# Loading the high parts of five weight chunks with a casting DMA from GpSimd instead of copying them on ScalarE

## What is computed

```python
kv = (rms_norm(h @ w_dkv)[..., :256] @ w_ukv).reshape(b, s, 16, 64 + 64)   # chunks ukv0, ukv1
k  = rope_tail(rms_norm(concat([k_nope, k_rope_of_all_heads]), k_gain), cos, sin)
q  = (rms_norm(h @ w_dq) @ w_uq).reshape(b, s, 16, 96)                     # chunks uq0 .. uq3
q  = rope_tail(rms_norm(q, q_gain), cos, sin)
logits = einsum('bqhd,bshd->bhqs', q, k) * 96 ** -0.5                      # 16 heads, masked by blocks of 64
out = einsum('bhqs,bshd->bqhd', softmax(logits), v)
h = h + out.reshape(b, s, 1024) @ w_o                                      # chunks bo0 .. bo3
h = h + square(relu(rms_norm(h) @ w_up)) @ w_down                          # chunks mlp1.u*, mlp1.d*
```

## Time and profile before

| | |
|---|---|
| time, median of 3 runs | 1129.64 us (1126.74 to 1129.78) |
| time of the profiled execution | 1127.46 us |
| its span, first to last instruction | 1125.7 us |
| TensorE's mean granted clock | 0.995 of full |
| TensorE busy | 1101.4 us, 98% |
| VectorE busy | 769.9 us, 68% |
| ScalarE busy | 601.3 us, 53% |
| GpSimd busy | 138.3 us, 12% |
| ScalarE's weight copies (line 1700) | 156 in one group, 290.1 us |

### The profile page before, as it was taken

One profiled execution on the slowest core, in us unless ns is written; L12 is line 12 of the kernel. 1 busy time (PEld: TensorE's weight loads), 2 busy tenths in 40 slices (PEclk: granted clock), 3 DMA queues, 4 the chain that ended last, 5 costly groups with the idle time before them and its releaser, 6 DMA issues.

```text
span 1125.7 us, 17842 instructions
## 1 busy us (share of the span) xinstructions
PE 1101.4 (98%) x7003; PEld 976.9 (87%) x7003; DVE 769.9 (68%) x1077; ACT 601.3 (53%) x778; POOL 138.3 (12%) x104
## 2 busy tenths in 40 slices
PE   8999999999999999999999999999999999999996
PEld 7868888888888888888889999898899989999995
DVE  6774665555668656565656878566688578988885
ACT  6574544444679555444455546455545357555552
POOL 3632100000275240000030000000000002000001
PEclk9999999999999999999999999999999999999998
DMA  9635565565342246656545654446643556654631
GB/s 344 237 115 114 177 200 194 183 201 187 107 146 96 76 130 224 198 188 193 187 151 185 202 169 127 145 150 215 216 155 127 165 209 225 218 174 170 223 131 38
DMA packets 138785, 194.00 MB, mean 172 GB/s; under 512 B 7147, under 2 KB 112840, under 8 KB 138716
## 3 DMA queue, kind: packets, MB, share of 16 engines
q1 hardware_dynamic: 126796, 181.92, 48.8%
q10 hardware_dynamic: 11312, 11.05, 3.5%
q0 software_dynamic: 608, 0.08, 0.0%
HBM read 191.90 MB, written 6.37 MB: 176 GB/s over the span
## 4 chain that ended last, share of the span: by engine, by line
PE 77%; DVE 7%; ACT 7%; DMA 4%; issue 3%; POOL 1%; SPq 0%; ACTq 0%; DVEq 0%; POOLq 0%
PE psum L616 19%; PE psum L617 19%; PE psum L618 19%; PE psum L825 9%; PE psum L826 5%; ACT arena L1686 4%; ACT whi L1700 2%; PE psum L704 2%; DMA skew_a<-tab_a 2%; DVE wlo L2314 2%; PE psum L1355 1%; PE psum L1382 1%; DMA raw<-in_a_w_in 1%; PE psum L734 1%; DVE arena L2840 1%
## 5 line engine op out<-in xcount | busy, mean ns | idle before, releaser
L2314 DVE TENSOR_TENSOR wlo<-raw,whi 128x2048 fp32r<-128x2048 f32 (+3 forms) x136 | 307.0, 2264 | 128.7 <-ACT whi L1700 127.7
L1700 ACT ACTIVATE whi<-raw 128x2048 fp32r<-128x2048 f32 (+3 forms) x156 | 290.1, 1868 | 187.1 <-PE psum L618 125.3
L616 PE MATMUL psum<-xA,whi 128*128 128x256 f32 x840 | 239.3, 285 | 0.1
L617 PE MATMUL psum<-xA,whi 128*128 128x256 f32 x840 | 237.6, 283 | 0.0
L618 PE MATMUL psum<-xA,wlo 128*128 128x256 f32 x840 | 237.6, 283 | 0.0
L1669 POOL TENSOR_TENSOR wlo<-raw,whi 128x288 fp32r<-128x288 f32 (+3 forms) x51 | 90.0, 1792 | 759.5 <-ACT whi L1700 759.4
L825 PE MATMUL psum<-xA,whi 128*128 128x512 f32 x512 | 181.9, 398 | 0.0
L616 PEld LDWEIGHTS psum<-xA,whi 128*128 128x128 f32 x840 | 160.3, 191 | 3.3 <-issue 1.2
L617 PEld LDWEIGHTS psum<-xA,whi 128*128 128x128 f32 x840 | 160.4, 191 | 1.1
L618 PEld LDWEIGHTS psum<-xA,wlo 128*128 128x128 f32 x840 | 160.3, 191 | 0.1
L826 PE MATMUL psum<-xA,wlo 128*128 128x256 f32 x512 | 143.7, 281 | 0.0
(11 more groups left out here) (302 smaller groups left out, 1673.5 us busy)
## 6 DMA issues: line engine op xcount, KB each, us to landing
raw<-in_w_in SPq DMA_DIRECT2D x42, 1024.0 KB, 4.9
raw<-in_mlp_w_up SPq DMA_DIRECT2D x32, 1024.0 KB, 5.2
raw<-in_mlp_w_down SPq DMA_DIRECT2D x32, 1024.0 KB, 4.8
raw<-in_w_gate SPq DMA_DIRECT2D x11, 1024.0 KB, 5.1
raw<-in_w_up SPq DMA_DIRECT2D x11, 1024.0 KB, 6.4
down_raw<-in_w_down SPq DMA_DIRECT2D x6, 1024.0 KB, 8.0
arena<-in_w_down SPq DMA_DIRECT2D x5, 1024.0 KB, 8.5
raw<-in_b_w_o SPq DMA_DIRECT2D x4, 1024.0 KB, 5.0
```

Of the source, the lines that this page charges most:

```text
L616: nc.tensor.matmul(out, lh, rh, start=start, stop=False, skip_group_check=skip)
L617: nc.tensor.matmul(out, lh, rl, start=False, stop=False, skip_group_check=skip)
L1700: nc.scalar.activation(whi[split_of[c]][:, 0:n], raw_bufs[raw_of[c]][:, 0:n], ACT.Copy).then_inc(hi_sem, 1)
L2314: V.tensor_tensor(wlo[split_of[c]][:, 0:n], raw_bufs[raw_of[c]][:, 0:n], f(whi[split_of[c]][:, 0:n]), ALU.subtract).then_inc(lo_sem["dve"], 1)
```

## The change

The five chunks uq2, uq3, bo0, bo1 and bo2 still come as they are by SP into `raw`. In addition GpSimd issues a second load of each from memory straight into the slot `whi`. The source is float32 and the destination float32r, so this load casts. ScalarE's copies of the five are gone. GpSimd's low part of these chunks waits for both loads and no longer for `hi_sem`. Each casting load waits, on GpSimd, for TensorE to have ended its work on the slot's last user. Where they stand in GpSimd's queue: uq2 ahead of `square_queries(0)`, uq3 after the low part of uq1, bo0 after the low part of uq2, bo1 after `scale_key_rope(1)`, bo2 after `square_queries(2)`.

```diff
+        cast_names = ("uq2", "uq3", "bo0", "bo1", "bo2")
...
-                high[c] = n_ring
+                n_high += chunk["name"] not in cast_names
+                high[c] = n_high
...
+        cast_sem = [sem(f"weight_high_landed{i}") for i in range(N_SPLIT)]
...
+        def high_ready(c):
+            return (cast_sem[split_of[c]], cast_count[c]) if c in cast_count else (hi_sem, high[c])
...
+            def cast_high(name):
+
+                c = index[name]
+                pool.wait_ge(*chunk_done[prev_split[c]])
+                (_, k, n, _, _, src), = chunks[c]["loads"]
+                pool.dma_start(whi[split_of[c]][:, 0:k * n].rearrange("p (k n) -> p k n", n=n), src).then_inc(
+                    cast_sem[split_of[c]], 16)
...
                 if chunks[c]["name"] == "uq1":
+                    cast_high("uq2")
                     square_queries(0)
                 if chunks[c]["name"] == "uq2":
+                    cast_high("uq3")
                     scale_key_rope(0)
+                if chunks[c]["name"] == "uq3":
+                    cast_high("bo0")
                 if chunks[c]["name"] == "bo0":
                     scale_key_rope(1)
+                    cast_high("bo1")
                     square_queries(1)
                     square_queries(2)
+                    cast_high("bo2")
...
-                pool.wait_ge(hi_sem, high[c])
+                if c in cast_count:
+                    pool.wait_ge(raw_sem[raw_of[c]], landed[c])
+                pool.wait_ge(*high_ready(c))
...
                     c = next_split[0]
+                    if c in cast_count:
+                        next_split[0] += 1
+                        continue
```

More of the change, by code:

```diff
@@ L298, in program @@
         last_raw, last_split = {}, {}
-        n_ring, at_split, turn_of = 0, N_SPLIT - 1, None
+        cast_names = ("uq2", "uq3", "bo0", "bo1", "bo2")
+        n_ring, n_high, at_split, turn_of = 0, 0, N_SPLIT - 1, None
         for c in range(NC):
@@ L324, in program @@
             landed[c] = count[raw_of[c]]
+        cast_sem = [sem(f"weight_high_landed{i}") for i in range(N_SPLIT)]
+        cast_n, cast_count = [0] * N_SPLIT, {}
+        for name in cast_names:
+            c = index[name]
+            cast_n[split_of[c]] += 16
+            cast_count[c] = cast_n[split_of[c]]
+        def high_ready(c):
+            return (cast_sem[split_of[c]], cast_count[c]) if c in cast_count else (hi_sem, high[c])
         chunk_done = {}
```

## The result

The changed kernel took 1140.71 us, median of 4 runs (1139.77 to 1141.36); the kernel before, beside it, 1128.95 us (1126.74 to 1129.78). The ratio is 1.0107, with a 95% interval of 1.0095 to 1.0119: 1.1% slower. The forecast was 1132.3 us, at most 1137.0.

The account below looks back on a forecast made before the run. The prediction took TensorE, busy 1101.4 of 1125.7 us, as the bound. The head loop starting 3.28 us later, less 0.63 us gained, made +2.65 us on the median 1129.64: 1132.3 us, range 1127.0 to 1137.0.

Parts of the forecast that it names:

- The fifth issue (bo2): GpSimd, behind the third query squares: bo2's casting-load issue costs nothing; 0.91 us if that cover went.
- The queue: GpSimd up to the third query squares: 2.18 us new waiting plus 3.84 issues less 2.46 old waits, 3.56 us later.
- The gain of 0.63 us: Head loop: VectorE's 0.63 us wait at 371.77 for ScalarE's first high part goes, shortening TensorE's later wait equally.
- The whole sum: Whole kernel: head loop starts 3.28 us later, less 0.63 us gained: +2.65 us, 1132.3 us, +0.23%.
- B: Casting load is dear: issues at twice the estimate, +6.5 us, 1136.1, or late landing, +4.35 us, 1134.0; chance 0.27.
- A: The prediction's own sum, +2.65 us, 1132.3 us, range 1130.4 to 1132.9; chance 0.50.
- C: ScalarE paces the head loop, so all three bo copies count, 5.76 us: -2.48 us, 1127.2; chance 0.13.
- D: GpSimd's delay is absorbed, for instance by VectorE waits taken as fixed: 0 to -0.6 us, about 1129.3; chance 0.10.

Follow-up runs that it names:

- e4: The changed kernel with casting loads for uq2 and uq3 alone, the bo chunks copied by ScalarE as before: 1131.03 us, ratio 1.002.
- e5: The changed kernel with bo2's casting load issued behind GpSimd's low parts of bo0 and bo1 instead of right ahead of them: 1133.8 us, ratio 1.0053.
- e7: The changed kernel, with each GpSimd low-part instruction of a bo chunk waiting for the one before it to end: 1133.41 us, ratio 1.0047.
- e8: The changed kernel with VectorE's additions of both pairs given to ScalarE's square root as its bias: 1131.35 us, ratio 1.0024.
- e2: The kernel before, no casting load, ScalarE's copies of bo0 and bo1 put early so their low parts follow the squares: 1132.23 us, ratio 1.0028.
- e1: The changed kernel, with GpSimd's low part of bo0 made to wait until VectorE's query means are done: 1131.76 us, ratio 1.0023.
- e11: The changed kernel with casting loads for bo0 to bo2 only, all three issued behind the third query squares: 1128.18 us, ratio 0.9996.
- e9: The changed kernel with bo2's casting load issued ahead of the third query squares, not behind them: 1133.66 us, ratio 1.0051.
- e10: The kernel of e2 plus a plain 1 MB load into a spare buffer, issued by GpSimd between the squares and the run: 1138.15 us, ratio 1.0077.
- e3: The changed kernel with casting loads for bo0, bo1 and bo2 alone, uq2 and uq3 copied by ScalarE as before: 1139.3 us, ratio 1.0083.
- e6: The kernel of e2 with bo2 alone by a casting load, issued between the squares and the run: 1139.84 us, ratio 1.0099.

## Why the prediction was wrong

**The step that failed** is this one: "The fifth issue (bo2) stands behind them; the low parts of bo0 to bo2 follow, still earlier than the 355.73 of before, so it costs nothing." It asked who waits for these low parts (nobody), and not what else runs while they do. At 355.73 they had lain beside the heads; now the issue and the run stand beside VectorE's two additions, on the way to the first maximum. That step cost nearly all of the +8.57 us between the third squares and the first maximum (where the forecast had -0.28). The heads took +1.07 us (where it had -0.63). The forecast had no term for the clock, which fell there. It falls in e4, e5, e7 and e8 too, where the means aren't held past 2 us, so this part is not shown to come from the hold. By e2 a run alone takes the pair of additions from 0.50 to 1.98 us; the issue ahead of it takes them to 9.33.

**What is shown of the cause.** All lengths are of the same pair of 128x12 additions on VectorE; alone it takes 0.50 us.

| kernel | on GpSimd ahead of the run of low parts | pair, us |
|---|---|---|
| the kernel before, e1, e4 | the run starts after the additions | 0.50 |
| e11 | three issues; the run starts after the additions | 0.67 |
| e2 | squares | 1.98 |
| e5 | squares (last issue four squares earlier) | 1.97 |
| e9 | issue, two squares | 1.96 |
| e7 | issue; pauses inside the run | 1.87 |
| e10 | plain issue | 9.37 |
| the changed kernel | casting issue | 9.33 |
| e3, e6 | casting issue | 10.29, 10.31 |

The pair of 128x4 additions beside the low part of uq3 says the same a second time. Where bo0's issue stands right ahead of it (the changed kernel, e1, e5, e7, e9) it takes 3.65 to 3.66 us; where none does, 1.03 to 1.34 us (the kernel before, e2, e3, e4, e6, e10, e11; in e3 a wait of 0.90 us lies between).

So: a load that GpSimd issues right ahead of a run of its own SBUF instructions, with no pause, keeps VectorE's SBUF-to-SBUF TENSOR_SCALAR out over many of them; without the issue it is let in after one. Excluded are the run by itself (e2), the cast (e10), the transfer under way (e5, e10), and, in the executions traced, an issue a little earlier with squares behind it (e5, e9).

**A pause ends it.** GpSimd's squares and key-rope instructions each wait for the one before, by a semaphore of their own; its low parts don't. The trace of the changed kernel shows the pause: the two key-rope instructions at 342.31 last 1.035 and 1.046 us and take 2.16 us together, so 0.08 us lie between them; four squares of 0.83 us take 3.56. Held against the pauses, the cases fall into line:

```profile
332.76 1.54 DVE L2778 TENSOR_SCALAR st<-st 128x8 f32<-128x8 f32 x1
L1640 POOL TENSOR_TENSOR arena<-arena,st x2: 1035/1040/1046, 342.3 to 343.4; 128x512 f32<-128x512 f32 x2
```

- Beside uq3 four low parts and one key-rope instruction follow bo0's issue without a pause. The first addition gets in at 343.37, and the first pause begins at 342.31 + 1.035 = 343.35.
- The key's addition at 332.76 meets uq3's issue, behind which the first key-rope instruction and a pause stand. It is held to 334.30, for one instruction.
- In e9 each of the two squares after the issue is followed by a pause, in e3 a wait of 0.90 us follows bo0's issue, and in e7 the pauses stand in the run. In all three the pair takes no longer than beside a run with no issue ahead of it.

So a pause fits all of these, and a number of instructions doesn't. Only e7 was made to show it; the rest is read from the traces afterwards.

The Trainium skill (SBUF — State Buffer, Who interferes with whom) has the first half: a tensor_scalar in a two-port mode and a GpSimd instruction exclude each other for one whole instruction, whoever issues first, and a tensor_reduce never takes part. The trace agrees on the reductions (0.55 us each beside the run too) and in e2 on the one instruction. By that rule the changed kernel would have had about e2's 1.98 us here (an estimate); it measured 9.33, and the measurement decides.

**What stays open** is why the hold ends without a pause. In all four kernels with the 128x12 pair held, the first addition got in at the end of the eighth low part, after 9.06 to 9.10 us. In the changed kernel and e10 no low part follows there at once; in e3 and e6 a ninth does, with no gap. Eight instructions, or some 9 us, could be a limit of its own: in all four the addition starts at the same point of the run, so no run here tells these apart. Nor is it known what the issue changes that a run by itself doesn't.

**What was right.** The queue: 3.56 us of delay forecast, 3.63 measured. Its terms were off and made up for each other: the first issue started at 326.66, 2.66 us after the 324.0 at which GpSimd went on before (sum: 2.18), the four issues took 0.83 + 0.82 + 0.76 + 0.76 = 3.17 us (sum: 3.84), and ahead of bo1's issue stands a pause of 0.30 us that the sum did not have. 2.66 + 3.17 + 0.30 - 2.46 = 3.67. The gain of 0.63 us was 0.59 by e11. The whole sum, +0.23%, is e1's ratio, once the additions are out of the way. That the delay came within 0.07 us is partly luck, since its terms were each off by 0.3 to 0.7 us.

**The rivals.** None of the four reached the measured time; the dearest, B with doubled issues, gave 1136.1 us. A was the right sum with a step missing. B fell: an issue costs 0.76 to 0.83 us, below the estimate of 0.91 to 1.01, and in the changed kernel GpSimd waits for no cast (in e4 0.24 us for that of uq3). Their times from issue to landing in the changed kernel:

```profile
whi<-in_b_w_o POOLq DMA_DIRECT2D x3, 1024.0 KB, 7.9
...
whi<-in_b_w_uq POOLq DMA_DIRECT2D x2, 576.0 KB, 5.7
```

The trap that the Trainium skill names (SBUF — State Buffer, the "DVE blocks DMA" trap), that descriptors aren't written while VectorE holds the port, doesn't show in the issues: e11's three took 2.24 us, 0.75 each, with VectorE's sums and additions beside them. (No run shows whether these additions held the port.) What showed is a hold in the other direction, on VectorE. C fell by e11: of the 5.76 us of copies 0.59 counted. D fell: the 3.63 us went through to the sums, which started at 349.21, 0.10 us after the squares.

## What to carry to other kernels

When work on GpSimd moves, ask which VectorE instructions it will lie beside: an SBUF-to-SBUF TENSOR_SCALAR of 0.25 us on the critical path can be held for a whole run, above all when a load issued by GpSimd stands right ahead of that run. Put pauses into the run (e7) or instructions with pauses between issue and run (e9, with the one long execution in mind), the run behind the critical instruction (e1), or the small addition into another engine's bias (e8). A held instruction counts as busy, so look for it as a longest duration far above its line's median, and as one long piece of the chain.

## What the runs showed of the hardware that was not expected

- One VectorE instruction of 128x12 values took 9.06 us instead of about 0.25 us beside GpSimd's run, if a GpSimd load was issued right ahead of the run; 1.98 us for two if not. Plain and casting loads do the same (9.37 and 9.33 us for the pair).
- The hold ended at GpSimd's first pause of 0.08 us between two instructions (343.35, addition let in at 343.37), and, where none came, after 9.06 to 9.10 us, with the eighth instruction.
- Casting costs nothing that shows at the issue: 0.74 to 0.79 us for 1024 KB with the cast, 0.79 without; 0.81 to 0.83 for 576 KB in more rows.
- After 8.86 us of TensorE without work the granted clock was 0.64 in the next 10 us. But in e4 it was 0.83 in the same stretch with no wait of TensorE over 1.62 us in the 20 us ahead of it, and in e1, with waits as long, 1.00. The heads up to the second subtraction took 30.95 us in the changed kernel, 30.54 to 30.74 in e4, e5, e7 and e8, and 29.29 to 29.36 at a clock of 1.00 (e1, e2, e11). What makes the clock fall in some of them the runs don't show.
